# Norm rows, first products and rounding pieces in another order at the seams of a two-block transformer kernel

## The reference, cut to what matters

```python
for layer in range(DEPTH):                       # first block
    sh1, sc1, g1, sh2, sc2, g2 = jnp.split(mod, 6, axis=-1)
    mix = _mixer(x * (1.0 + sc1) + sh1, ...)      # ends with the product by w_out
    x = _layernorm(DEEPNORM_ALPHA * x + (1.0 + g1) * mix, ln1_g[layer], ln1_b[layer])
    u = x * (1.0 + sc2) + sh2
    ff = _dense_swiglu(u, ...) if layer % 2 == 0 else _moe_swiglu(u, ...)
    x = _layernorm(DEEPNORM_ALPHA * x + (1.0 + g2) * ff, ln2_g[layer], ln2_b[layer])
for i in range(DEPTH):                           # second block
    x = post_norm(x, 0.5 * swiglu(x, ffn1_w_in[i], ffn1_w_out[i]), ln_g[i, 0], ln_b[i, 0])
    x = post_norm(x, mix, ln_g[i, 1], ln_b[i, 1])  # mix = attention, ends with the product by w_o
    x = post_norm(x, 0.5 * swiglu(x, ffn2_w_in[i], ffn2_w_out[i]), ln_g[i, 2], ln_b[i, 2])
    ...                                           # gated embedding and its norm
```

## Time and profile before

| | |
|---|---|
| median of 3 runs | 2583.55 us (2577.95 to 2587.95) |
| the profiled execution | 2577.67 us, span 2575.9 us |
| busy: PE, DVE, ACT, POOL | 2448.4 us (95%), 1705.0 (66%), 1303.3 (51%), 113.5 (4%) |
| chain that ended last | PE 83%, DVE 9%, DMA 3%, ACT 3%, issue 2%, POOL 1% |
| mean granted TensorE clock | 0.988 of full speed |

### The profile page before, as it was taken

One profiled execution on the slowest core, in us unless ns is written; L12 is line 12 of the kernel. 1 busy time (PEld: TensorE's weight loads), 2 busy tenths in 40 slices (PEclk: granted clock), 3 DMA queues, 4 the chain that ended last, 5 costly groups with the idle time before them and its releaser, 6 DMA issues.

```text
span 2575.9 us, 31571 instructions
## 1 busy us (share of the span) xinstructions
PE 2448.4 (95%) x11660; PEld 1942.6 (75%) x11660; DVE 1705.0 (66%) x1959; ACT 1303.3 (51%) x1658; POOL 113.5 (4%) x125
## 2 busy tenths in 40 slices
PE   7989997989999999999998999999998999999996
PEld 4657875658888888888876888768876887897884
DVE  2575454579999999999986545665455553556455
ACT  2324433338877878878873443544433443443442
POOL 1020001020000000000001000000000000000001
PEclk9999998999999999999998999999999999999998
DMA  9865548739999999999985553365535553336550
GB/s 367 306 217 168 195 186 316 272 99 378 389 336 384 364 322 382 364 329 380 361 304 192 179 196 113 110 210 180 177 119 196 196 172 115 121 124 216 195 179 33
DMA packets 316384, 608.11 MB, mean 236 GB/s; under 512 B 15105, under 2 KB 154401, under 8 KB 309602
## 3 DMA queue, kind: packets, MB, share of 16 engines
q1 hardware_dynamic: 308736, 581.04, 63.5%
q0 software_dynamic: 7248, 24.35, 2.8%
q10 hardware_dynamic: 274, 1.05, 0.1%
HBM read 605.31 MB, written 1.08 MB: 235 GB/s over the span
## 4 chain that ended last, share of the span: by engine, by line
PE 83%; DVE 9%; DMA 3%; ACT 3%; issue 2%; POOL 1%; DVEq 0%; ACTq 0%; SPq 0%
PE G L908 48%; PE A L908 27%; PE TB L908 4%; DMA down<-in_ada_w 1%; PE TB L1239 1%; DVE w_lo L2652 1%; POOL small L2453 1%; PE TB L930 1%; DVE u_lo L2932 1%; PE TB L1346 1%; DVE small L3005 1%; DMA down<-in_moe_w_down 1%; DMA wide<-in_ffn_w_in 1%; DVE l_lo L3285 0%; DVE x_tok L2994 0%
## 5 line engine op out<-in xcount | busy, mean ns | idle before, releaser
L908 PE MATMUL G<-w_hi,u_hi 128*128 128x512 f32 x1584 | 629.5, 397 | 10.1 <-DVE u_lo L2932 4.8
L908 PE MATMUL G<-w_hi,u_lo 128*128 128x512 f32 x1584 | 619.0, 391 | 0.0
L908 PE MATMUL G<-w_lo,u_hi 128*128 128x512 f32 x1584 | 618.8, 391 | 0.0
L2693 DVE TENSOR_TENSOR w_lo<-wide,w_hi 128x1024 fp32r<-128x1024 f32 x352 | 415.4, 1222 | 12.9 <-ACT w_hi L2037 3.7
L2037 ACT ACTIVATE w_hi<-wide 128x1024 fp32r<-128x1024 f32 x352 | 371.3, 1062 | 89.8 <-PE G L908 42.8
L908 PEld LDWEIGHTS G<-w_hi,u_hi 128*128 128x128 f32 x1584 | 298.6, 189 | 74.4 <-DVE w_lo L2652 9.2
L908 PEld LDWEIGHTS G<-w_hi,u_lo 128*128 128x128 f32 x1584 | 298.3, 188 | 64.6
L908 PEld LDWEIGHTS G<-w_lo,u_hi 128*128 128x128 f32 x1584 | 298.8, 189 | 59.7 <-issue 0.2
L908 PE MATMUL A<-w_hi,hidden_hi 128*128 128x512 f32 x772 | 301.4, 390 | 0.0
L908 PE MATMUL A<-w_hi,hidden_lo 128*128 128x512 f32 x772 | 300.7, 389 | 0.0
L908 PE MATMUL A<-w_lo,hidden_hi 128*128 128x512 f32 x772 | 300.5, 389 | 0.0
(11 more groups left out here) (379 smaller groups left out, 3200.8 us busy)
## 6 DMA issues: line engine op xcount, KB each, us to landing
down<-in_moe_w_down SPq DMA_DIRECT2D x176, 512.0 KB, 8.2
wide<-in_ffn_w_in SPq DMA_DIRECT2D x88, 1024.0 KB, 7.6
wide<-in_moe_w_gate SPq DMA_DIRECT2D x160, 512.0 KB, 8.4
wide<-in_moe_w_up SPq DMA_DIRECT2D x160, 512.0 KB, 9.1
down<-in_ffn_w_out SPq DMA_DIRECT2D x44, 1024.0 KB, 8.7
down<-in_ada_w SPq DMA_DIRECT2D x40, 1024.0 KB, 7.0
wide<-in_w_in SPq DMA_DIRECT2D x24, 1024.0 KB, 8.3
wide<-in_fox_w_in SPq DMA_DIRECT2D x12, 1024.0 KB, 5.3
```

The source lines that it names most:

```text
L908: return nc.tensor.matmul(o, lhsT, rhs, start=start, stop=stop, skip_group_check=True)
L2693: V.tensor_tensor(w_lo[at % RING][:, :], raw_piece(n, at)[0], w_hi[at % RING][:, :].bitcast(F32), ALU.subtract).then_inc(lo_ready, 1)
```

## The change

Five things are changed.

1. The fold leaves GpSimd. Three VectorE operations at the head of `woven_norm` do the same, and `folded` waits for two signals instead of one.
2. At the output seams (`by_tile`) `early_rest` moves: `w_lo` pieces 0 and 1 behind tile 0's norm, pieces 2 and 3 behind tile 1's.
3. `up_by_tile` becomes `first_up`, in all dense layers: for tile 0 first all hi x hi products, then those with `u_lo`, then those with `w_lo`. The first wait for `w_hi` and `u_hi` only. At the output seams (`late`: O1, O3, O4) the tile 0 products with `w_lo` pieces 2 and 3 are put into tile 1's, behind its first two pieces. Tile 1's transposes stand behind tile 0's products.
4. At the same seams ScalarE and VectorE do the second unit's pieces 0 and 1 ahead of tile 0's silu and product.
5. `CLOCK_FILL` loses 12 fills: 9 from (3, 2, 0) to (0, 2, 0), 31 from (4, 0, 0) to none, 47 from (3, 0, 2) to none.

```diff
-CLOCK_FILL = {5: (3, 0, 2), 9: (3, 2, 0), 16: (3, 0, 2), 20: (2, 9, 0), 24: (3, 0, 0),
-              27: (1, 6, 0), 31: (4, 0, 0), 34: (1, 0, 0), 37: (4, 5, 0), 39: (0, 0, 1), 47: (3, 0, 2),
+CLOCK_FILL = {5: (3, 0, 2), 9: (0, 2, 0), 16: (3, 0, 2), 20: (2, 9, 0), 24: (3, 0, 0),
+              27: (1, 6, 0), 31: (0, 0, 0), 34: (1, 0, 0), 37: (4, 5, 0), 39: (0, 0, 1), 47: (0, 0, 0),
...
+    def late_order(i):
+
+        return plan[i][0] == "ffn" and any(plan[j][0] in ("out1", "out2") for j in (i - 3, i - 4))
...
+                def first_rounded(t, q):
+
+                    if t == 0:
+                        pe.wait_ge(hi_ready, n.lo + q + 1)
+                        if q == 0:
+                            open_g(n.g + 1)
+                    if q % 2 == 0:
+                        pe.wait_ge(act_ready, n.act - 4 + 2 * t + q // 2 + 1)
+                    first_pass(t, q, uhv, w_hi, start=True)
+
+                def first_low(t, q):
+
+                    if q % 2 == 0:
+                        pe.wait_ge(t_evac, n.tg - 3 + 2 * t + q // 2)
+                    return first_pass(t, q, ulv, w_hi, stop=t == 1)
+
+                def first_weight_low(t, q):
+
+                    if t == 0:
+                        pe.wait_ge(lo_ready, n.lo + q + 1)
+                    last = first_pass(t, q, uhv, w_lo, stop=t == 0)
+                    if t == 0 and q == 3:
+                        last.then_inc(g_done, 1)
+
+                def first_up():
+
+                    for q in range(4):
+                        first_rounded(0, q)
+                    for q in range(4):
+                        first_low(0, q)
+                    for q in range(2 if late else 4):
+                        first_weight_low(0, q)
+                    if second_half:
+                        second_half()
+                    for q in range(4):
+                        if late and q == 2:
+                            first_weight_low(0, 2)
+                            first_weight_low(0, 3)
+                        first_rounded(1, q)
+                        first_weight_low(1, q)
+                        first_low(1, q).then_inc(g_done if q == 3 else up_used, 1)
...
-                    up_by_tile(j, c) if j == 0 else up(j, c)
+                    first_up() if j == 0 else up(j, c)
...
-                        silu(c, 0)
+                        if not late:
+                            silu(c, 0)
                         piece(1, c + 1, 0)
                         piece(1, c + 1, 1)
+                        if late:
+                            silu(c, 0)
                         silu(c, 1)
...
-                link(V.tensor_scalar(mod[:, 4, :], mod[:, 4, :], 1.0, None, ALU.add))
-                link(V.tensor_tensor(mod[:, 0, :], lnp[:, D:2 * D], mod[:, 4, :], ALU.mult))
-                link(V.tensor_tensor(mod[:, 3, :], mod[:, 3, :], mod[:, 0, :], ALU.add))
-                V.tensor_tensor(mod[:, 4, :], mod[:, 4, :], lnp[:, 0:D], ALU.mult).then_inc(norm_folded, 1)
...
+            def fold(n):
+
+                dve.wait_ge(s_ln, 32 * (n.ln + 1))
+                dve.wait_ge(rows_in, 32 * (2 * (n.ln // 2) + 2))
+                link(V.scalar_tensor_tensor(out=mod[:, 0, :], in0=mod[:, 4, :], scalar=1.0, in1=lnp[:, D:2 * D],
+                                            op0=ALU.add, op1=ALU.mult))
+                V.tensor_tensor(mod[:, 3, :], mod[:, 3, :], mod[:, 0, :], ALU.add).then_inc(norm_folded, 1)
+                V.scalar_tensor_tensor(out=mod[:, 4, :], in0=mod[:, 4, :], scalar=1.0, in1=lnp[:, 0:D],
+                                       op0=ALU.add, op1=ALU.mult).then_inc(norm_folded, 1)
...
-                if before != "moe" and not split_in_tail(index - 1):
+                if row is not None:
+                    fold(n)
+                if before != "moe" and not by_tile and not split_in_tail(index - 1):
                     early_rest(behind, 0)
-                    if not by_tile:
-                        early_rest(behind, 1)
+                    early_rest(behind, 1)
...
                 if by_tile:
-                    early_rest(behind, 1)
+                    early_rest(behind, 0)
                     lower_half("trs8", trs, 0, 2)
...
+                if by_tile:
+                    early_rest(behind, 1)
                 lower_half("trs8", trs, 2, 2)
```

54 lines of the change are left out of this document (18 added, 36 removed).

## The result

| | before | changed |
|---|---|---|
| median | 2583.55 us (2577.95 to 2587.95) | 2570.46 us (2568.53 to 2571.69) |
| ratio to before | | 0.9949, 95% interval 0.9932 to 0.9966 |
| span of the profiled execution | 2575.9 us | 2567.8 us |
| mean granted clock in it | 0.988 | 0.986 |

The medians are of five runs each; the changed kernel is faster by 13.1 us, 0.51%, with an interval of 8.8 to 17.6 us. A second set of five runs on another occasion gave 2570.11 us and the same ratio (0.9936 to 0.9962, or 9.8 to 16.5 us). The prediction was 2569.5.

A forecast was written before the change was run, and what follows sets the result against it. TensorE was taken as the bound almost everywhere, so only seams between layers could move the time. Terms summed to 15.9 us, less 1.8 for the clock, rounded to 14.0 off the median 2583.55: 2569.5 us, range 2560 to 2580.

The forecast's parts named there:

- rival 2: First two output seams: slow pieces have another cause or the fold eats its slack; 7.5 us gained, 2576.0; chance 0.08.
- rival 4: Third unit's weights: w_lo pieces 2 and 3 free their slot late; 4.9 us slower, 2588.4; chance 0.05.
- rival 1: Three longer waits of TensorE each end in a clock fall costing 1.6 us; 11.1 gained, 2572.4; chance 0.14.
- rival 3: ScalarE late: second unit's pieces ahead of first silu cost 1.3 us at three output seams; 10.1 gained, 2573.5; chance 0.07.
- The fold: First two output seams (stages 6 to 10, 17 to 21): with GpSimd quiet, TensorE's excess goes, 3.4 and 3.2 us.
- the slack of 2.3 us: Ahead of tile 0's norm, first output seam: the moved fold costs nothing while these 2.3 us hold; second seam alike.
- O1, the rest: First output seam, stages 6 to 10: tile 1's norm starts 5.5 us earlier, 0.7 given back; 4.8 us gained.
- O3: Third output seam, stages 29 to 32: tile 1's norm starts 3.4 us earlier, 0.7 given back; 2.7 us gained.
- O4: Fourth output seam, stages 45 to 48: tile 1's norm 3.7 us earlier, 0.9 more behind it; 4.6 us gained.
- the tails: From tile 1's norm start to first hidden transposes: 16.9 us at first output seam, 15.6 at third and fourth.
- E and K: Stages 23 to 25, behind the experts: 0.6 us gained (0 to 1.6); stages 38 to 40: 0, products only reordered.
- The clock: Longer TensorE waits for tile 1 lower the clock: 1.0 us lost at O4, 0.4 each at O1 and O3; 1.8.

The follow-up runs named there:

- fills_in_wait: The changed kernel with seven more clock fills, all inside TensorE's wait for tile 1's norm at three output seams; 2566.35 us, ratio 0.9937 to the kernel before.

## Why the prediction was right

The total alone decides little: the intervals of the two sets of runs, 8.8 to 17.6 and 9.8 to 16.5 us, leave out rival 2's 7.5 and rival 4, but hold rival 1's 11.1 and, with it, rival 3's 10.1. The stretches decide.

**The fold.** Predicted 3.4 us at O1 and 3.2 at O2; measured 3.1 to 3.6 and 3.1 (the time from out_hi to the norm). Mechanism and size stand, and the slack of 2.3 us is the wait of 2.31. The value of 1.2 us for the three new operations, from its nearest row, was 1.22.

**O1, the rest; O3; O4.** Without the clock, from fills_in_wait, the seams are 5.0, 2.8 and 4.9 us shorter than before, where the sum had 4.8, 2.7 and 4.6. The steps hold too: tile 1's norm starts 5.7, 4.0 and 3.5 us earlier behind out_hi at O1, O4 and O3 (predicted 5.5, 3.7 and 3.4), and without a fall the tails were right to 0.02 us. The tail was summed as 15.6 us at O3 and O4; the prediction's last paragraph has 15.7 for it. The experiments show what each part carries: pieces behind the norm 2.5 at O3 and O4 before the clock's part but only 0.6 at O1; moved products 1.9 at O3 and 2.3 at O4; the fills' removal 2.3, 3.4 and 0.3; pieces ahead of silu some 0.5 each. These overlap, so they do not add up to the whole.

**E and K.** Predicted 0.6 at E, measured 0.36 (-0.1 to 0.9 over the nine executions with the change's order there). The last u_lo does end 0.5 us earlier behind the residual in each of them, but VectorE's idle time behind the branch is 4.4 to 5.3 us, a scatter larger than the term. That one pair came near the 0.6 is luck. At K the predicted 0 holds: the stretch to O4 is 578.5 to 578.7 us in the changed kernels without a fall in it, 578.6 before.

**The clock.** Predicted 1.8 us, one fall at O4 and less than even odds at O1 and O3; measured 2.4, a fall at all three. A clock of 0.50 behind tile 1's transposes at O1 or O3 was one of the prediction's own signs of being wrong, and it came. Tile 1's waits were 2.17, 2.33 and 2.95 us against the predicted 2.5, 2.6 and 3.5. This is rival 1 in its mechanism, but a fall costs 0.6 to 0.9 us here and not 1.6, since part of it lies beside the wait for u_lo. The odds were too low: with all executions of the study, such a wait had a fall behind it 17 times in 25. More falls at a lower price came out near fewer at a higher one; that the term is off by only 0.6 is partly luck.

**The sum.** 15.9 - 1.8, rounded to 14.0, predicted; 13.7 at the seams, 13.1 in the medians. What the prediction did not have is that falls elsewhere move too. They made the spans of the two profiled executions differ by only 8.1 us, and a forecast set on the profiled execution of before (2563.7) would have been 6.8 us off. To put the terms on the median was the right choice.

**Rivals 2 to 4.** The fold did not stay in the way. ScalarE is not late; undoing the order costs time. The late slot passes nothing on: the stretches from the hidden transposes to the next seam, which hold the units whose load starts later, are 321.4 and 230.7 us behind O1 and O4 against 321.5 and 230.6. Behind O3 it is 580.4 against 578.6 with a fall of the clock, and 578.5 in fills_in_wait, which has the same late slot and no fall. Nothing in a run was made to test rival 4 by itself.
